# A hybrid trunk on one core: the order of the opening is changed

## The reference

```python
def rmsnorm(x, g):
    xf = x.astype(jnp.float32)
    y = xf * lax.rsqrt(jnp.mean(xf * xf, axis=-1, keepdims=True) + EPS)
    return (y * g.astype(jnp.float32)).astype(x.dtype)
...
    sh1, sc1, g1, sh2, sc2, g2 = jnp.split(mod[:, None, :].astype(x.dtype), N_MOD, axis=-1)
    h = rmsnorm(x, p['norm1_g']) * (1 + sc1) + sh1
    u, q, k, v, z, xbc, dt_raw = split_sizes(h @ p['w_in'], IN_SIZES)
...
        mod_ctx = jax.nn.silu(c_ctx)[None, :] @ w_mod[l] + b_mod[l]
```

## Time and profile before

| | us |
|---|---|
| median of 3 runs | 1304.84 (1304.83 to 1304.99) |
| the profiled execution | 1304.73, its span 1302.9 |
| PE busy | 1283.7 (99%) |
| PE weight loads | 1235.5 (95%) |
| DVE busy | 1080.5 (83%) |
| ACT busy | 652.2 (50%) |
| POOL busy | 185.6 (14%) |

### The profile page before, as it was taken

The page is one execution under the profiler, slowest core; times in us unless marked ns, Lnnn a source line. Parts: engine busy times, 40 slices in busy tenths (PEclk is TensorE's granted clock), DMA queues, the critical chain, the costliest instruction groups (busy, mean ns, idle before and its releaser), DMA issues.

```text
span 1302.9 us, 20244 instructions
## 1 busy us (share of the span) xinstructions
PE 1283.7 (99%) x7620; PEld 1235.5 (95%) x7620; DVE 1080.5 (83%) x2015; ACT 652.2 (50%) x1102; POOL 185.6 (14%) x188
## 2 busy tenths in 40 slices
PE   7999999999999999999999999999999999999997
PEld 6999889999999999999999988899999999999997
DVE  6899878878987999999968998887888899899433
ACT  5643555555566454443365336655455654544331
POOL 0077000002210000000103910001042000000101
PEclk9999999999999999999999999999999999999999
DMA  9566345554443444457735562564435254444441
GB/s 362 197 226 221 136 141 183 184 165 136 149 146 117 143 161 156 152 188 262 239 106 191 200 208 83 185 219 147 146 129 194 81 167 141 162 140 160 133 134 49
DMA packets 60625, 216.26 MB, mean 166 GB/s; under 512 B 7120, under 2 KB 9552, under 8 KB 58992
## 3 DMA queue, kind: packets, MB, share of 16 engines
q1 hardware_dynamic: 56512, 199.57, 44.7%
q0 software_dynamic: 4016, 15.39, 3.9%
HBM read 211.17 MB, written 3.77 MB: 165 GB/s over the span
## 4 chain that ended last, share of the span: by engine, by line
PE 78%; DVE 12%; ACT 6%; issue 3%; DMA 1%; SPq 1%; DVEq 0%; ACTq 0%
PE acc L1003 24%; PE acc L1004 23%; PE acc L1005 23%; DVE cv L1935 2%; DVE wl L1754 2%; DVE junk_late L1843 1%; PE mix L1172 1%; DMA head<-in_whead_dram 1%; ACT th L1387 1%; ACT hh L1376 1%; PE mix L1257 1%; PE mix L1200 1%; DVE ee L2063 1%; PE mix L1186 1%; DVE hl L1759 1%
## 5 line engine op out<-in xcount | busy, mean ns | idle before, releaser
L1003 PE MATMUL acc<-hh,wh 128*128 128x384 f32 x1519 | 516.6, 340 | 1.4 <-DVE hl L1759 0.6
L1005 PE MATMUL acc<-hh,wl 128*128 128x384 f32 x1519 | 507.9, 334 | 0.0
L1004 PE MATMUL acc<-hl,wh 128*128 128x384 f32 x1519 | 507.7, 334 | 0.0
L1754 DVE TENSOR_TENSOR wl<-raw,wh 128x1024 fp32r<-128x1024 f32 (+1 forms) x276 | 341.9, 1240 | 62.5 <-ACT wh L1351 61.2
L1351 ACT ACTIVATE wh<-raw 128x1024 fp32r<-128x1024 f32 (+1 forms) x276 | 286.8, 1040 | 133.3 <-PE acc L1005 130.7
L1003 PEld LDWEIGHTS acc<-hh,wh 128*128 128x128 f32 x1519 | 285.3, 188 | 8.5 <-issue 3.1
L1004 PEld LDWEIGHTS acc<-hl,wh 128*128 128x128 f32 x1519 | 285.3, 188 | 1.6
L1005 PEld LDWEIGHTS acc<-hh,wl 128*128 128x128 f32 x1519 | 285.1, 188 | 0.0
L1935 DVE SCALAR_TENSOR_TENSOR cv<-acc,prm,cv 128x1 f32<-128x1 f32 (+1 forms) x416 | 153.6, 411 | 9.0 <-ACT cv L1514 1.9
L1005 PE MATMUL acc<-ah,wl 128*128 128x384 f32 x352 | 117.6, 334 | 0.0
L1003 PE MATMUL acc<-ah,wh 128*128 128x384 f32 x352 | 117.6, 334 | 0.0
(11 more groups left out here) (313 smaller groups left out, 1695.0 us busy)
## 6 DMA issues: line engine op xcount, KB each, us to landing
raw<-in_wstream_dram SPq DMA_DIRECT2D x248, 512.0 KB, 3.5
rawm<-in_wstream_dram SPq DMA_DIRECT2D x80, 512.0 KB, 4.3
raw<-in_wstream_dram SPq DMA_DIRECT2D x32, 448.0 KB, 3.3
head<-in_whead_dram SPq DMA_DIRECT2D x8, 1024.0 KB, 15.9
rowf<-runs_dram POOLq DMA_DIRECT2D x12, 256.0 KB, 4.3
rowb<-runs_dram POOLq DMA_DIRECT2D x12, 256.0 KB, 4.8
crow_late<-in_cvec_rows_dram POOLq DMA_DIRECT2D x2, 1024.0 KB, 6.2
crow<-in_cvec_rows_dram POOLq DMA_DIRECT2D x2, 1024.0 KB, 5.3
```

What stands on the lines that cost most here:

```text
L1003: mm(out, sh, mhi, start=start, stop=False)
L1004: mm(out, sh, mlo, start=False, stop=False)
L1005: return mm(out, sl, mhi, start=False, stop=stop)
L1754: tt(wl[:, s, 0:n], raw[:, raw_slot(u), 0:n], wh[:, s, 0:n].bitcast(F32), ALU.subtract).then_inc(lo_done, 1)
```

## The change

The diff changes only the opening. SP issues `xs` and `xp` ahead of head tile 0. GpSimd adds the squares of tiles 0 and 1, and of 2 and 3, in place (`SQ_PAIRS`); PE sums six tiles instead of eight, those of 4 to 7 first, and does so ahead of `shift_products(0)`. In `first_joint` two thirds of tile 0's high products stand ahead of `head_transposes(2)`, and each later tile one step sooner against the head work; `shift_products(7)` goes ahead of `scale_products(6)`. ACT does `inv_rms` and `head_part(0)` ahead of `hi` of units 0 and 1. DVE makes only two tiles of `first_full` ahead of `head_scale(0)`, and takes `lo(0)` and `lo(1)` behind it.

```diff
@@ -86,6 +86,7 @@
 MOD_G2 = 5 * KT
 PE_SCALE = (2, 4, 6)
 DVE_AFFINE = (5, 7)
+SQ_PAIRS = (0, 2)
 NWT = 2
 UP0 = U_OF[(UP, 0, 0)]
 DOWN0 = U_OF[(DOWN, 0, 0)]
@@ -504,6 +505,7 @@
         z_ss = sem("z_ss")
         zeroed = sem("zeroed")
         sq_done = sem("sq_done")
+        sq_pair = sem("sq_pair")
         sq_sum = sem("sq_sum")
         sq_last = sem("sq_last")
         prescaled = sem("prescaled")
@@ -644,9 +646,9 @@
                 sp.dma_start(head[:, 2 * j:2 * j + 2, :], whead[j].rearrange("p (a c) -> p a c", a=2)) \
                     .then_inc(head_in[j], 16)
 
-            load_head(0)
             sp.dma_start(x[:, :, 0:LAT], xs).then_inc(x_in, 16)
             sp.dma_start(x[:, :, CTX0:T], xp).then_inc(x_in, 16)
+            load_head(0)
             load_head(1)
             for i, (l, kind, u) in enumerate(STREAM):
                 if i == JOINT:
@@ -767,6 +769,9 @@
                     row = runs_dram[l, r0:r0 + 4, :].rearrange("h t -> (h t)")
                     pool.dma_start(bank[:, :], row.partition_broadcast(P)).then_inc(rows_in[d], 16)
 
+            for i, j in enumerate(SQ_PAIRS):
+                pool.wait_ge(sq_done, j + 2)
+                nc.gpsimd.tensor_tensor(sq0[:, j, :], sq0[:, j, :], sq0[:, j + 1, :], ALU.add).then_inc(sq_pair, 1)
             pool.wait_ge(head_done, KT // 2)
             pool.dma_start(fg[:, :], fng).then_inc(fg_in, 16)
             for l in range(DEPTH):
@@ -938,35 +943,44 @@
                 def low_product(k, i):
                     return mm(acc[i][:, 0:T], weights(i, k)[0], hl[:, k, :], start=False, stop=(k == KT - 1))
 
+                def low_products(k):
+                    pe.wait_ge(h_lo, count(0, NSPLIT, SP_N1 + k))
+                    for i in range(JOINT):
+                        last = low_product(k, i)
+                        if i == 0 and k == KT - 3:
+                            last.then_inc(joint_left, 1)
+
                 def tile(k, between=None):
-                    if k == 0:
-                        for i in range(JOINT):
-                            wait_lo(pe, i)
                     pe.wait_ge(h_hi, count(0, NSPLIT, SP_N1 + k))
                     for i in range(JOINT):
                         high_products(k, i)
                     if between is not None:
                         head_sums(between)
-                    pe.wait_ge(h_lo, count(0, NSPLIT, SP_N1 + k))
-                    for i in range(JOINT):
-                        last = low_product(k, i)
-                        if i == 0 and k == KT - 3:
-                            last.then_inc(joint_left, 1)
-
-                for p in range(1, KT // 2):
-                    j = 2 * p
-                    if j in PE_SCALE:
-                        head_transposes(j)
-                        shift_products(j)
-                        if p > 1:
-                            tile(j - 3)
-                        scale_products(j)
-                        shift_products(j + 1).then_inc(part_done, 1)
-                    else:
-                        shift_products(j)
-                        shift_products(j + 1).then_inc(part_done, 1)
-                        tile(j - 3)
-                    tile(j - 2, between=p)
+                    low_products(k)
+
+                pe.wait_ge(h_hi, count(0, NSPLIT, SP_N1))
+                for i in range(2):
+                    wait_lo(pe, i)
+                    high_products(0, i)
+                head_transposes(2)
+                shift_products(2)
+                wait_lo(pe, 2)
+                high_products(0, 2)
+                low_products(0)
+                scale_products(2)
+                shift_products(3).then_inc(part_done, 1)
+                tile(1, between=1)
+                head_transposes(4)
+                shift_products(4)
+                tile(2)
+                scale_products(4)
+                shift_products(5).then_inc(part_done, 1)
+                tile(3, between=2)
+                head_transposes(6)
+                shift_products(6)
+                shift_products(7)
+                scale_products(6).then_inc(part_done, 1)
+                tile(4, between=3)
                 tile(KT - 3)
 
                 k = KT - 1
@@ -986,9 +1000,12 @@
 
             def first_squares():
 
-                for j in range(KT):
+                for j in range(4, KT):
                     pe.wait_ge(sq_done, j + 1)
-                    last = mm(mz, ones, sq0[:, j, :], start=(j == 0), stop=(j == KT - 1))
+                    mm(mz, ones, sq0[:, j, :], start=(j == 4), stop=False)
+                for i, j in enumerate(SQ_PAIRS):
+                    pe.wait_ge(sq_pair, i + 1)
+                    last = mm(mz, ones, sq0[:, j, :], start=False, stop=(j == SQ_PAIRS[-1]))
                 last.then_inc(misc_done, 1)
 
             def misc_turn(l, i):
@@ -1305,8 +1322,8 @@
 
             pe.wait_ge(ones_in, 16)
             conditioning_rows()
+            first_squares()
             shift_products(0)
-            first_squares()
             shift_products(1).then_inc(part_done, 1)
             head_sums(0)
             first_joint()
@@ -1422,17 +1439,16 @@
             def first_norm():
 
                 transposed(2)
-                first_high(0)
+                first_high(1)
                 head_part(1)
-                first_high(1)
+                first_high(2)
                 transposed(4)
-                first_high(2)
+                first_high(3)
                 head_part(2)
-                first_high(3)
+                transposed(6)
                 first_high(4)
+                head_part(3)
                 first_high(5)
-                transposed(6)
-                head_part(3)
                 first_high(6)
                 first_high(7)
 
@@ -1656,14 +1672,15 @@
             act.wait_ge(ones_in, 16)
             for l in range(DEPTH):
                 if l == 0:
+                    inv_rms(l, 0, D)
+                    head_part(0)
                     hi(l, 0)
                     hi(l, 1)
-                inv_rms(l, 0, D)
-                if l == 0:
-                    head_part(0)
+                    first_high(0)
                     hi(l, 2)
                     first_norm()
                 else:
+                    inv_rms(l, 0, D)
                     norm(l, 0)
                 for u in range(NU):
                     if u == UP0:
@@ -2212,24 +2229,27 @@
                     row(1)
                     scale_sum(0, 1)
                     scale_sums(1)
+                    dve.wait_ge(rs_ready, 1)
+                    first_full(0)
+                    first_full(1)
+                    head_scale(0)
                     lo(l, 0)
                     lo(l, 1)
-                    dve.wait_ge(rs_ready, 1)
-                    for j in range(4):
-                        first_full(j)
-                    head_scale(0)
+                    first_low(0)
                     lo(l, 2)
-                    first_low(0)
-                    scale_sums(3)
+                    first_full(2)
+                    first_full(3)
+                    scale_sum(3, 0)
                     first_low(1)
+                    scale_sum(3, 1)
+                    head_scale(1)
                     first_full(4)
-                    head_scale(1)
                     first_full(5)
+                    first_low(2)
                     scale_sums(5)
-                    first_low(2)
+                    first_low(3)
+                    head_scale(2)
                     first_full(6)
-                    head_scale(2)
-                    first_low(3)
                     dve.wait_ge(scale_ready, 3)
                     first_affine(5)
                     first_full(7)
```

## The result

The changed kernel takes 1308.77 us (median of 9 runs, 1307.93 to 1309.41) against 1304.84 us (9 runs, 1304.57 to 1305.48): a ratio of 1.0027, with a 95% interval of 1.0018 to 1.0036. It is 3.9 us slower. The forecast was 1306.8 with a range up to 1308.0, so the result lies outside it, on the slow side. The profiled execution of the changed kernel took 1308.41 us.

The account below looks back on a forecast made before the run. The opening was taken as bound by PE's work and clock from 20.78 us. A joint 0.9 us later plus 1.2 of later waits, +2.1 on 1304.73, gave 1306.8; range 1304.0 to 1308.0.

Parts of the forecast that it names:

- The sum: Opening: PE's joint from 21.0 plus 6.6 work and 2.3 clock gives 29.9 at head tile 4's transposes, +0.9; later waits +1.2.
- The wait that takes the place of the one removed: DVE's sums and second `row` wait for head tile 0 landing at 11.5, ending at 17.9 instead of 17.00: 0.9 us.
- The clock behind that point: PE at 1.2 GHz from its first joint product at 21.0 until 25.67: 4.7 us, 2.3 lost.
- The shift is carried one to one: The opening's delay of 2.1 us was taken to reach the end of the kernel in full.
- one such tile earlier: Token data ahead of head tile 0 land one 1 MB tile's 2.5 us sooner, at 9.4 instead of 11.9.
- 1.7 us of before's 6.5: Of PE's 6.5 us from 20.78 to head tile 4's transposes, 1.7 was counted lost to the clock, leaving 4.8 work.
- Nothing of PE's work had come ahead of 20.78: PE, before busy from 20.78, now starts the joint at 21.0, though `hh` 0 comes at 20.9 instead of 24.1.
- The terms given for tile 2: About 2.2 us from `head_sums(1)` on, against PE's 0.6 low products, 1.0 transposes, 0.6 shifts: stall of about 0.3.
- The waits behind the transposes of head tile 4: Lost cover in the joint: stalls of 0.3 at tile 2, 0.6 at tile 4, 0.3 in the last two; together 1.2.
- Rival (a): PE's clock is up at 21 and stays up: 2.3 us back, 1304.5, or 1303.4 to 1304.1 with shorter waits; chance 0.25.
- Rival (b): PE's low-clock level lasts one stretch longer, until 29.1: another 1.7 us, 1308.5; chance 0.11.
- Rival (c): Loads share all engines, so token data land with head tile 0 at 11.9; `hh` 0 at 22.5, 1308.3; chance 0.05.

Follow-up runs that it names:

- both fills: Changed kernel with nine unused PE products ahead of the squares and 14 more between `head_sums(0)` and `first_joint()`: 1306.56 us, and 1306.38 in a second batch.
- the first filling: Changed kernel with nine unused PE products between `conditioning_rows` and `first_squares`: 1308.44 us.
- eight squares on PE: Changed kernel without GpSimd's additions, PE summing all eight squares in order: 1308.03 us.
- the old order put back: Changed kernel with `first_joint`, `first_norm` and four `first_full` ahead of `head_scale(0)` as before; loads, squares, additions, early 1/rms and late `lo(0)`, `lo(1)` stay: 1305.55 us.
- the load order alone: Kernel before with only the load order changed, token data ahead of head tile 0: 1305.38 us.
- tile 1's high products earlier: Kernel before with six unused PE products ahead of `head_sums(0)`, and `tile(1)`'s high products ahead of `head_transposes(4)`: 1304.40 us.
- the load order put back: Changed kernel with head tile 0 issued ahead of the token data again: 1310.43 us.
- one load for the token data: The kernel of tile 1's high products earlier, with `xs` and `xp` in one array loaded by one DMA in 12 KB rows: 1303.28 us.
- filling of the kernel before: Kernel before with six unused PE products ahead of `head_sums(0)`: 1304.59 us.
- the order alone: Kernel before with only the new order of `first_joint`, `first_norm` and DVE; `lo(0)` and `lo(1)` stay ahead of the tiles: 1309.72 us.

## Why the prediction was wrong

**The step that failed.** The sum starts PE's joint at 21.0, on an `hh` 0 that is there at 20.9. It is there at 23.1, and PE starts at 23.16. The wait that takes the place of the one removed, DVE's sums behind head tile 0, was named, but put at 17.9 and is 19.43; the rest comes through the squares and ACT's queue, below. The clock behind that point, put at 2.3 us, was too dear, which hides 0.7 of the 2.2.

**The sum.** The transposes of head tile 4 were put at 29.9 against 29.0; they start at 31.33, so +2.3 instead of +0.9. The joint starts 2.2 late, and takes 31.33 - 23.16 = 8.2 us to that point instead of 8.9. Behind them the joint takes 49.52 - 31.33 = 18.19 us, against 45.93 - 27.25 - 1.78 = 16.90: +1.3, forecast 1.2. The shift is carried one to one, as said. The failure lies ahead of the joint, and has three parts, which follow.

**A low stretch that the prediction did not have.** It dated the squares on PE from square 4, and did not ask what PE does until then. The old order took square 0 as soon as it came; the new one leaves PE idle 2.20 us, and the products run at the low clock: 1.13 us a product (4.52 us for eight instructions, which are four products) instead of 0.68. The squares end at 18.2 instead of 15.7, and `rs` is there at 19.5 instead of 16.8. With the clock up, in the trace with both fills, the squares end at 16.6 and `rs` is there at 17.9, so 1.6 us of this are the clock. The length of the idle time does not by itself decide whether the stretch comes. It is absent behind 0.52 and 0.70 us (the first filling, eight squares on PE), but also behind 2.92 (the old order put back) and 2.94 (the load order alone, where the shift products came in between), and present behind 3.32 (tile 1's high products earlier) and 5.02 (the load order put back). Most of what it costs here is hidden, because DVE is late as well: in the trace with both fills, with head tile 0 landing at the same time, the joint starts at 22.70 instead of 23.16, which is 0.46. It is the work that ACT has behind `rs` that comes late, below.

**The wait for head tile 0.** The mechanism was right and the size was not. Head tile 0 lands at 12.7, outside the bounds of 10.7 to 12.0, and DVE's first sum beside GpSimd's second addition takes 1.55 us instead of 1.23; its last sum ends at 19.43 instead of 17.9 (17.00 before). What failed is "one such tile earlier", which took every load at the same rate. The queue's first loads are now the token data, in rows of 1 KB and 512 bytes, where it was a head tile in rows of 8 KB: windows 3 to 4 and 4 to 5 moved 127 and 182 GB/s against 243 and 319 before, and the loads behind are 0.6 to 0.8 us late (PE gets head tile 2 at 21.34 and 21.39 in the old order put back and the load order alone, and had it at 20.78 before). So the token data land at 10.2 instead of 9.4. The load order alone on the kernel before gives the same picture, 122 and 207 GB/s, so it is the order that does it. The rows' length as the cause is likely but not shown by itself. The run with one load for the token data has head tile 0 in front, and gains 444 against 378 GB/s only in 5 to 9 us; it changes the number of loads too.

The Trainium skill, page "DMA: Bandwidth & Descriptors", section "Why small descriptors are slow (HBM only)", gives a fixed overhead of about 3 cycles per packet at 32 bytes per cycle. As an estimate by that page this is 9% for rows of 1 KB and 19% for 512 B. The trace agrees in size in 5 to 9 us, where 378 GB/s are 15% less than 444. It does not explain the two windows at the start, where the rates are 43 to 48% below before's while the DMA share is 0.40 and 0.60 against 1.31 and 0.80: there the 16 engines were not kept busy, and no run here shows what held them back.

Of the contention on DVE the Trainium skill, page "GPSIMD Engine Reference", section "8. Key points", says that GpSimd shares its SBUF interfaces with VectorE and that instructions with two SBUF inputs are hit; the 1.55 us of this sum, which reads two tensors, against 1.23 agrees. Without GpSimd's additions, in the run with eight squares on PE, it takes 1.23.

**ACT's queue.** `hh` 0 was put 1.5 us behind `head_scale(0)`, at 20.9. It comes at 23.1: 1.5 from DVE's late last sum, 0.2 from the steps up to `head_scale(0)`, which ends at 21.02, and 0.5 because ACT has `hi(0)` and `hi(1)`, 1.99 us together, in front of `first_high(0)`. With `rs` at 16.8 they would have been over in time; with `rs` at 19.5 they run until 21.6. PE's joint starts at 23.16 instead of 21.0.

**The clock behind it.** The stretch was put at 21.0 to 25.67 with 2.3 us lost. It was at about 22.7 to 26.1, and by the traces with and without fills it costs 31.33 - 23.16 less 29.77 - 22.70, that is 1.1 us. With the clock up those steps took 7.1 us, where the sum had 6.6 of work, so short waits make up 0.5. With the 0.46 of the first stretch this makes 1.6 in the two profiled executions, 2.2 to 2.4 in the medians. Where the low stretches lie may differ from one execution to the next, and that the fills shrink the spread of the runs from 1.5 to 0.4 us fits this, but only one execution of each kernel has a trace.

**What before had lost.** The sum took off 1.7 us of before's 6.5 as clock that a new order could escape. The filling of the kernel before shows that this was no loss: its PE timeline is then 0.3 us ahead at the same point behind the joint (45.62 for 45.93), the median 0.2 less, because head tile landings and `hh` hold PE instead. A low clock costs nothing where PE at full speed would only arrive early at its next wait. This also tells why the new order is dear: before, PE filled the time until `hh` 0 with the transposes and shifts of head tile 2, which needs only a load. The new order puts products of `hh` ahead of them, and PE stands idle 2.71 us until 23.16; with the old order put back it starts at 21.34. Of the 3.9 us, 3.2 go with the order, by that run. The parts don't add up: the order alone on the kernel before costs 4.9, the loads alone at most a little (0.6 between medians), since each moves what the other waits for.

**What held.** Nothing of PE's work had come ahead of 20.78. GpSimd's additions were hidden on PE's side, and shorter than assumed (0.98 us each, for 1.45), but they gave nothing. The waits behind the transposes of head tile 4 sum to about the forecast: 0.2 at tile 2 (0.3), 0.77 at tile 4 (0.6), 0.50 in the last two (0.3). Rival (a), the clock up from 21 us, would have needed the filling, and even with it the time is 1306.4 to 1306.6, not 1304.5. Rival (b), a longer low stretch, is what the first filling, the order alone and the old order put back showed. Rival (c) came near in time, but its reason was wrong: token data and head tile 0 land 2.5 us apart.

**Slips in the working.** A low stretch left at 22.26 to 25.67 costs 1.7 us, so the sum with it would be 0.6 us less and not 0.3. The terms given for tile 2 balance (2.2 us against 0.6 + 1.0 + 0.6), and don't yield the stall of 0.3 that was put. The two lower times of rival (a) are 1303.3 and 1303.9 by its own sum. None of these decides the outcome.

**Open.** Why the first low stretch is absent in some executions and present in others isn't settled. Nor is why the token data land up to 0.8 us later in some, but it goes with SP: with head tile 0 in front they land at 11.9, 12.2, 12.7 and 12.8 us where SP is held by the DMA issue behind them for 3.16, 3.49, 3.94 and 3.91.

## What to carry to other kernels

Work that needs only a load belongs in front of work that needs a chain of three engines, even if the second is the dearer product: putting the product first left PE idle for 2.7 us here. Before counting a low-clock stretch as a loss, ask what PE would wait for at full speed; a handful of unused products in the idle time answers that in one run. When loads change places at the start of a queue, don't price them by their bytes alone: here those in short rows moved about half the rate there.

## What the runs showed of the hardware

A reordering that starts an engine later can cost twice: in the changed kernel PE's products ran at 1.2 GHz behind 2.20 us of idle time, at a place where nothing had been slow before. It is not certain to, since in two other versions the same place was at full speed behind 2.9 us. Nor is it bound to the new order: the kernel before with six fills and the one with tile 1's high products earlier have the same instructions on PE up to and with the squares, which took 5.43 us in the one execution and 7.12 in the other. The column of the granted clock doesn't tell everything at the start: in the kernel before it reads 1.00 up to 8 us, but products of the same form take 421 ns until 8.0 us and 275 ns from 8.4 on (line, engine, operation and count: shortest, median and longest in ns, first and last start); what makes the first ones slower is not shown:

```profile
L877 PE MATMUL acc<-tb,cpad x12: 421/421/421, 5.6 to 8.0; 128*128 128x128 f32 x12
```

```profile
L877 PE MATMUL acc<-tb,cpad x12: 275/275/387, 8.4 to 9.7; 128*128 128x128 f32 x12
```

The issue of a DMA behind the two short-row loads holds SP for 3.16 us, and for up to 3.94 in other executions; behind the one load in long rows it takes 0.43.
